# Two layers of a hybrid attention block: later turns of the attention outputs, the last two of them inside the first out-projection unit, and sums over the output weights taken three units ahead

## The chip, the cores and the metric

The kernel runs on one core of a Trainium2 chip. The metric is the device time of one execution in microseconds (us), the median of three runs. The profile below is of one further execution.

## What is computed

The reference is a backbone block of a latent generator, two layers deep, on 512 latent tokens and 256 context tokens of width 1024. Cut to what matters here:

```python
def trunk_layer(x, xt, ...):
    h  = modulate(rms_norm(x,  g_attn), sh_a,  sc_a)
    ht = modulate(rms_norm(xt, g_attn), tsh_a, tsc_a)
    q_w,k_w,v_w, q_n,k_n,v_n, q_g,k_g,v_g = split_mixer_inputs(h @ w_in, qk_g)     # groups A, B, C
    ...                                                  # the same for the context, rotary on A and C
    o = concatenate([window_attention(A), neighbourhood_attention(B), global_block_attention(C)])
    x = x + ga_a * (o @ w_out)                           # the output projection
    x = x + ga_f * swiglu(modulate(rms_norm(x, g_ffn), sh_f, sc_f), w_gate, w_up, w_down)
    if update_ctx:                                       # first layer only
        ot = concatenate([context_attention(A), context_attention(B), context_attention(C)])
        xt = xt + tga_a * (ot @ w_out)
        xt = xt + tga_f * swiglu(...)
    return x, xt
```

There are 16 heads of 64: A has 6 (windowed, with a sink logit), B has 4 (neighbourhood, with a bias), C has 6 (global). Layer 0 works on latent and context tokens (768), layer 1 on the latent ones alone (512).

## The kernel before, in words

The program is one instruction stream for each engine, written out by hand, with semaphores between the streams. Each layer goes through norm, input projection, attention, output projection and FFN. The change touches the attention and the output projection; the FFN behind them begins when the residual of the output projection is complete and normed.

**Attention** is a sequence of steps, each one query block of one head: 96 in layer 0 (0 to 23 group A on latent tokens, 24 to 35 A on the context, 36 to 59 C latent, 60 to 79 C and B on the context, 80 to 95 B latent) and 64 in layer 1 (0 to 23 A, 24 to 47 C, 48 to 63 B). For step g, PE computes scores (`score`, L1158 and L1159), DVE takes their top (`top_of`, L1940 for the bias of B, L1943), DVE in layer 0 (L1950) and POOL in layer 1 (L768) turn it into an offset, ACT takes the exponential (`softmax`, L1506), PE transposes the probabilities two steps later (`turn`, L1175), ACT and DVE split them into a high and a low half (`turned_high` L1528, `turned_low` L1957) and PE weighs the values four steps later (`weigh`, L1190 and L1192). After every fourth step DVE sums the group (`sum_outputs`, L1965 and L1969) and POOL writes its high and low half (L799, L804, L809) and so releases `o_ready`.

**Turns.** The output projection needs the attention outputs with channels on partitions, in eight tiles m of 128 channels. `turn_output` (L1207) transposes tile m on PE: 8 transposes for the latent part (part 0), 4 for the context part (part 1, layer 0 only), into one of three PSUM banks that the steps' own transposes use too. ACT copies them out in `take_turned` (L1564; for tiles 3 and 4, part 0, two copies that also permute, L1560) and releases `ot_taken`. The table `OUT_TURNS` gives each turn the step at which PE and ACT issue it, behind that step's own work. Tiles 0, 1, 2 hold group A, 3 and 4 group B, 5 to 7 group C.

**The output projection** has eight units j (an output tile of 128 columns), each of eight contraction tiles in the order `OUT_ORDER` (0, 1, 2, 5, 6, 7, 3, 4), six matmuls each in layer 0 and three in layer 1 (L1262). Its weights come as float32 and are split in two f16 halves with a scale of their own for each unit: ACT squares and sums unit j's weights (`square_out`, L1541), PE adds the sums over the partitions (`sum_out`, L1243; for the first `N_OUT_EARLY` units in one go, L1229), DVE makes the scale (`scale_out`, L1976 to L1982), ACT rounds the high half (`round_out`, L1548), POOL scales and subtracts for the low half (`split_out`, L716 and L719). Before the change the first three units are squared and rounded within the steps, and unit 0 is split by POOL among its last output writes; the rest follows during the units, `sum_out(j + 2)` behind the first tile of unit j. The raw weights of units 3 to 7 are loaded to where attention buffers were, once the last `o_ready` is out.

After unit 0 PE bounds the activations (L1267), and after units 2 and 3 it adds the weight sums of the first two FFN weight pairs (`sum_weights`, L1014), for which ACT squares in `first_pairs` (L1597), DVE scales in `scale_weights` (L2036 to L2043) and ACT rounds (L1608). DVE adds the residual (L1790) and the squares for the next norm (`add_square`, L1719), ACT squares the residual (L1386). The last unit's norm sums are on PE at L954 and L960. Before the first unit's own squares ACT switches its table and warms the root (L1589).

## Time and profile before

| | before |
|---|---|
| median of 3 runs | 1812.2 us (1811.83 to 1812.23) |
| profiled execution | 1816.11 us |
| its span in the trace | 1814.3 us |
| mean granted TensorE clock | 0.972 |
| PE busy | 1683.0 us (93%) |
| DVE, ACT, POOL busy | 964.3, 714.1, 835.0 us |
| attention, layer 0 (first exponential to last value matmul) | 226.9 to 431.2 us |
| output projection, layer 0 | 434.98 to about 501 us |
| attention, layer 1 | 1230.7 to 1379.6 us |
| output projection, layer 1 | 1383.38 to about 1436.6 us |

Busy time is not time at full speed: a matmul that is issued while the clock is at half its speed is busy twice as long. A table by stage therefore has the granted clock beside the busy times. "Idle before, released by" says how long an engine stood before a group and which semaphore let it go.

### The profile page before, as it was taken

The numbers are of one execution on the slowest core, as the hardware profiler recorded it, in microseconds if no ns is written. First come the engines' busy times: TensorE is split into PE (matmuls) and PEld (weight loads), VectorE is DVE, ScalarE is ACT, GpSimd is POOL, SyncE is SP. The second block draws the span as 40 slices with busy tenths as digits, with TensorE's granted clock in tenths as the row PEclk, the third lists the DMA queues.
The fourth block names the chain that finished last, engine by engine and source line by source line (L and its number), as shares of the span: only waits on it lengthen the run. The fifth ranks groups of instructions, "written<-read, shape, count | busy, mean of one in ns | idle before, by whom it ended". The sixth has DMA issues, their size and how long they took to land. (4 is left out here: it accounts for less than half of the span.)

```text
span 1814.3 us, 28248 instructions
## 1 busy us (share of the span) xinstructions
PE 1683.0 (93%) x11087; PEld 1201.4 (66%) x11087; DVE 964.3 (53%) x1760; ACT 714.1 (39%) x1276; POOL 835.0 (46%) x656
## 2 busy tenths in 40 slices
PE   7999988977989999999899989997976899999998
PEld 3688877865656678667766778786764345645646
DVE  4544498884468841787238743457883522122112
ACT  3222278877443310332013112226886464053130
POOL 2244347784514452436314234532444557458463
PEclk9999989998989999999999989999998899999999
DMA  9344352322134423363315423533003224334332
GB/s 312 49 113 113 96 137 78 89 64 76 37 95 137 129 67 85 100 178 101 110 48 180 128 64 73 120 88 91 11 13 94 58 70 116 93 89 109 82 81 82
DMA packets 314353, 175.01 MB, mean 96 GB/s; under 512 B 87518, under 2 KB 309614, under 8 KB 314222
## 3 DMA queue, kind: packets, MB, share of 16 engines
q1 hardware_dynamic: 284686, 143.70, 30.5%
q10 hardware_dynamic: 29536, 29.51, 5.1%
q8 instruction: 89, 1.46, 0.3%
q14 instruction: 42, 0.34, 0.1%
HBM read 159.04 MB, written 2.83 MB: 89 GB/s over the span
## 5 line engine op out<-in xcount | busy, mean ns | idle before, releaser
L981 PE MATMUL acc<-act,pair_w 128*128 128x512 f16 x3168 | 582.2, 345 | 6.2 <-ACT act L1403 4.2
L981 PEld LDWEIGHTS acc<-act,pair_w 128*128 128x128 f16 x3168 | 307.8, 98 | 270.6 <-DVE act L1765 10.0
L981 PE MATMUL acc<-hidden,split_w 128*128 128x512 f32 (+1 forms) x1584 | 311.8, 358 | 10.7 <-issue 6.4
L981 PEld LDWEIGHTS acc<-hidden,split_w 128*128 128x128 f32 x1584 | 261.9, 189 | 58.0 <-issue 7.1
L706 POOL TENSOR_SCALAR split_w<-raw_w 128x1024 fp32r<-128x1024 f32 (+1 forms) x104 | 109.2, 1050 | 354.9 <-PE acc L981 274.4
L843 POOL TENSOR_SCALAR pair_raw<-pair_raw,weight_scale 128x1024 f32<-128x1024 f32 x88 | 106.6, 1212 | 357.2 <-ACT pair_w L1608 357.2
L981 PE MATMUL acc<-act,split_w 128*128 128x512 f32 x1344 | 261.4, 353 | 4.1 <-ACT act L1403 2.5
L709 POOL TENSOR_TENSOR split_w<-raw_w,split_w 128x1024 fp32r<-128x1024 f32 (+1 forms) x104 | 241.9, 2326 | 8.7
L981 PEld LDWEIGHTS acc<-act,split_w 128*128 128x128 f32 x1344 | 214.1, 190 | 39.6 <-issue 3.6
L2109 DVE SCALAR_TENSOR_TENSOR mod_acc<-mod_chunk,silu_c,mod_acc 128x256 f32<-128x256 f32 x280 | 230.3, 865 | 4.0
L846 POOL TENSOR_TENSOR pair_w<-pair_raw,pair_w 128x1024 f16<-128x1024 f32 x88 | 189.0, 2148 | 7.3
L2072 DVE SCALAR_TENSOR_TENSOR prod<-acc,weight_scale,silu_g 128x768 f32<-128x768 f32 (+1 forms) x44 | 38.9, 884 | 256.4 <-PE acc L981 251.2
L1597 ACT ACTIVATE squares_out<-pair_raw 128x1024 bf16<-128x1024 f32 x88 | 92.6, 1052 | 170.4 <-DMA pair_raw<-in_w_up 166.1
L1790 DVE SCALAR_TENSOR_TENSOR x_t<-acc,mod,x_t 128x512 f32<-128x512 f32 x72 | 45.2, 659 | 207.5 <-PE acc L981 206.9
L1506 ACT ACTIVATE prob<-acc,stat,score_scale 128x768 f32<-128x768 f32 (+5 forms) x160 | 131.2, 820 | 54.2 <-DVE stat L1950 26.5
L1653 ACT ACTIVATE hidden<-prod 128x768 fp32r<-128x768 f32 (+1 forms) x44 | 32.4, 737 | 242.2 <-DVE prod L2072 242.2
L1943 DVE TENSOR_REDUCE stat<-acc 128x1 f32<-128x768 f32 (+5 forms) x160 | 117.3, 733 | 15.4 <-PE acc L1159 10.3
L1190 PE MATMUL small<-v,prob_t 128*128 128x128 f16 x696 | 83.4, 224 | 32.6 <-DVE o_sum L1969 31.5
L1262 PE MATMUL acc<-out,out_w 128*128 128x512 f16 x576 | 111.8, 355 | 1.0 <-POOL out_w L719 1.0
L1158 PE MATMUL acc<-ks,qs 128*128 128x256 f16 (+1 forms) x384 | 92.5, 272 | 20.0 <-ACT prob L1506 19.1
L1608 ACT ACTIVATE pair_w<-pair_raw,weight_scale 128x1024 f16<-128x1024 f32 x88 | 95.9, 1136 | 7.6 <-DVE weight_scale L2043 7.6
L1957 DVE TENSOR_TENSOR prob_t<-side,prob_t 128x512 f16<-128x512 f32 (+2 forms) x157 | 86.6, 567 | 21.4 <-ACT prob_t L1528 19.9
(216 smaller groups left out, 2141.9 us busy)
## 6 DMA issues: line engine op xcount, KB each, us to landing
mod_chunk<-in_w_mod ACTq DMA_DIRECT2D x28, 1024.0 KB, 5.2
pair_raw<-in_w_gate SPq DMA_DIRECT2D x44, 512.0 KB, 4.0
pair_raw<-in_w_up SPq DMA_DIRECT2D x44, 512.0 KB, 5.4
raw_w<-in_w_in SPq DMA_DIRECT2D x64, 256.0 KB, 3.7
raw_w<-in_w_down SPq DMA_DIRECT2D x32, 512.0 KB, 4.2
raw_w<-in_w_mod SPq DMA_DIRECT2D x24, 512.0 KB, 3.9
mod_start<-in_w_mod SPq DMA_DIRECT2D x8, 1024.0 KB, 11.4
ks<-q_split SPq DMA_DIRECT2D x64, 96.0 KB, 2.2
```

Of the source, the lines that this page charges most:

```text
L706: pool.tensor_scalar(split_w[slot][:, 0, 0:n, :], raw_w[slot][:, 0:n, :], 1.0, 0.0, ALU.mult, ALU.add).then_inc(hi_w, 1)
L709: pool.tensor_tensor(split_w[slot][:, 1, 0:n, :], raw_w[slot][:, 0:n, :], split_w[slot][:, 0, 0:n, :].bitcast(F32), ALU.subtract).then_inc ...
L843: pool.tensor_scalar(raw, raw, weight_scale[:, 1, 2 * f + s:2 * f + s + 1], 0.0, ALU.mult, ALU.add).then_inc(weight_mul, 1)
L846: pool.tensor_tensor(w[:, s, 1, :, :], raw, w[:, s, 0, :, :], ALU.subtract).then_inc(pair_ready, 1)
L981: mm = pe.matmul(acc[slot][:, a:b], weights[:, part == 2, k, :], moving[:, part == 1, k, a:b], start=(k == 0 and part == 0), stop=(k == n ...
L1158: pe.matmul(out_, q, ks[:, s["k"], 0, k0:k0 + size], start=True, stop=False)
L1262: mm = pe.matmul(acc[u % 2][:, a:b], out_w[j % 4][:, part == 2, k, :], out16[k][:, part == 1, a:b], start=(i == 0 and part == 0), stop=(i ...
L1506: sc.activation(prob[g % 3][:, 1 - s["sink"]:1 + n], src, ACT.Exp, bias=stat[:, 1, i:i + 1], scale=score_scale[:, 0, gi:gi + 1], accum_out ...
L1597: sc.activation(squares_out[:, :], pair_raw[home(f)][:, s, :, :].rearrange("p k n -> p (k n)"), ACT.Square, accum_out=weight_sum[:, 2 * f ...
L1608: sc.activation(pair_w[home(f)][:, s, 0, :, :], pair_raw[home(f)][:, s, :, :], ACT.Copy, scale=weight_scale[:, 1, 2 * f + s:2 * f + s + 1] ...
L1943: ve.reduce_max(stat[:, 0, i:i + 1], src, AX_X).then_inc(top, 1)
L2109: s = ve.scalar_tensor_tensor(**kw, in1=kw["out"], op0=ALU.mult, op1=ALU.add)
```

## The change: what it does, and the diff

It moves the turns of group A (tiles 0 to 2) from the C latent steps to the context steps in layer 0 and from the A and C steps to the first B steps in layer 1, and spreads the later ones anew. The turn of tile 3, part 0, now stands at the head of unit 0 and that of tile 4 in front of unit 0's seventh tile. Only two units' weights are summed together; in layer 1 their squares, scale, rounding and POOL's split now stand in the A steps, with a scratch tile of their own (`out_squares1`). The other sums stand one unit earlier: that of unit 2 behind unit 0's first tile, that of unit 3 in front of unit 0's seventh tile, that of unit j + 3 within unit j. The FFN's first two weight sums stand one unit later. The kernel's arithmetic is the same.

```diff
 OUT_TURNS = [
-    [(38, 0, 0), (40, 1, 0), (42, 2, 0), (47, 0, 1), (49, 1, 1), (51, 2, 1), (74, 5, 0), (75, 6, 0), (76, 7, 0),
-     (79, 5, 1), (83, 6, 1), (86, 7, 1), (90, 3, 1), (94, 4, 1), (99, 3, 0), (100, 4, 0)],
-    [(26, 0, 0), (29, 1, 0), (37, 2, 0), (50, 5, 0), (53, 6, 0), (60, 7, 0), (66, 3, 0), (68, 4, 0)],
+    [(60, 0, 0), (62, 1, 0), (64, 2, 0), (66, 0, 1), (68, 1, 1), (70, 2, 1), (74, 5, 0), (77, 6, 0), (80, 7, 0),
+     (82, 5, 1), (84, 6, 1), (87, 7, 1), (90, 3, 1), (95, 4, 1), (100, 3, 0), (100, 4, 0)],
+    [(48, 0, 0), (50, 1, 0), (52, 2, 0), (54, 5, 0), (57, 6, 0), (61, 7, 0), (68, 3, 0), (68, 4, 0)],
 ]
...
-OUT_SUM_STEP = [92, 56]
-OUT_SQUARE_STEP = [(88, 89, 90), (51, 52, 53)]
-OUT_ROUND_STEP = [(94, 95, 96), (58, 59, 61)]
-N_OUT_EARLY = 3
+OUT_SUM_STEP = [92, 6]
+OUT_SQUARE_STEP = [(88, 90), (2, 4)]
+OUT_ROUND_STEP = [(94, 97), (8, 10)]
+N_OUT_EARLY = 2
+N_OUT_SUMS = KT - N_OUT_EARLY + 1
...
+        out_squares1 = place("out_squares1", [P, 8 * P], BF16, split_at_ + 12288)
...
-            def split_out(l, j):
-
-                u = u_out(l) + j
+            def scale_raw(l, j):
+
                 pool.wait_ge(out_hi, KT * l + j + 1)
                 pool.tensor_scalar(out_raw[j][:, :, :], out_raw[j][:, :, :], out_scale[:, 1, j:j + 1], 0.0, ALU.mult, ALU.add
                                    ).then_inc(hi_w, 1)
+
+            def split_out(l, j):
+
+                u = u_out(l) + j
                 pool.wait_ge(hi_w, ring_of[u] + 1)
...
-                    if i == 4 * N_GROUPS[l]:
+                    if i == 14:
+                        scale_raw(l, 0)
+                    if i == 18:
                         split_out(l, 0)
...
-                for n, m, part in turns_at(l, g1 + 4 - g0):
-                    turn_output(n, m, part)
+                last_two = turns_at(l, g1 + 4 - g0)
 
                 def sum_out(j):
 
+                    if j == 2:
+                        pe.wait_ge(o_summed, sum(N_GROUPS[:l + 1]))
                     pe.wait_ge(out_sq, KT * l + j + 1)
...
                     for i, k in enumerate(OUT_ORDER):
+                        if j == 0 and i in (0, KT - 2):
+                            turn_output(*last_two[i // 6])
                         if j == 0:
                             pe.wait_ge(ot_taken, last_turn[k])
-                        if 1 <= j < KT - 2 and i == 1:
-                            sum_out(j + 2)
+                        if j == 0 and i in (1, KT - 2):
+                            sum_out(2 + i // 6)
+                        if 1 <= j < KT - 3 and i == 1:
+                            sum_out(j + 3)
...
-                    if j in (2, 3):
-                        sum_weights(l, j - 2)
+                    if j in (3, 4):
+                        sum_weights(l, j - 3)
...
-                    if j == 0:
+                    if l == 0 and j == 0 or l and j == 2:
                         sc.wait_ge(scores, LAYER_STEPS[l][-16] + 1)
+                    elif l and j == 0:
+                        sc.wait_ge(unit_done, u_in(l) + 16)
...
                     for n, m, part in turns_at(l, g - g0):
                         take_turned(n, m, part)
+                    if g == g1 + 1:
+                        square_out(2)
...
                 def first_pairs(k):
                     if k == 0:
+                        round_out(2)
                         square_out(3)
-                    elif k + 2 < KT:
-                        round_out(k + 2)
                     if k + 4 < KT:
                         square_out(k + 4)
-                    if k in (1, 2):
-                        square_pair(k - 1)
-                    if k in (4, 5):
-                        round_pair(k - 4)
+                    if k + 3 < KT:
+                        round_out(k + 3)
+                    if k in (2, 3):
+                        square_pair(k - 2)
+                    if k in (5, 6):
+                        round_pair(k - 5)
...
-                    if 1 <= j < KT - 2:
-                        scale_out(j + 2, j + 3, small[:, j + 2:j + 3])
+                    for i in ((2, 3) if j == 0 else (j + 3,) if j < KT - 3 else ()):
+                        scale_out(i, i + 1, small[:, i:i + 1])
...
-                    if j in (2, 3):
-                        scale_weights(j - 2)
+                    if j in (3, 4):
+                        scale_weights(j - 3)
```

**PE, end of the attention and unit 0 in layer 0, before.** The names are `out_0` to `out_7` for the eight turned tiles, `o` for the attention outputs, `out_w` for the split weights; "..." stands for the same six matmuls on the tiles between.

```order
L1207 MATMUL side<-ident_h,o_132 128x128 [waits o_ready,prob_lo]
L1207 MATMUL side<-ident_h,o_132 128x128 x7
L1207 MATMUL mod_ps<-ident_h,o_132 128x128 [waits o_ready,prob_lo]
L1207 MATMUL mod_ps<-ident_h,o_132 128x128 x7
L1262 MATMUL acc<-out_0_133,out_w_54 128x512 [waits ot_taken,split_ready,exps]
...
L1262 MATMUL acc<-out_1_134,out_w_54 128x512 [waits ot_taken]
...
L1262 MATMUL acc<-out_4_137,out_w_54 128x256
L1267 MATMUL mod_ps<-act_scale,ones 128x1 [waits bound_step]
L1262 MATMUL acc<-out_0_133,out_w_55 128x512 [waits split_ready]
...
L1243 MATMUL small<-out_sum,ones_69 128x1 [waits out_read,out_sq]
```

The same place after the change:

```order
L1216 MATMUL side<-ident_h,o_132 128x128 [waits ot_taken,o_ready,split_ready,exps]
L1216 MATMUL side<-ident_h,o_132 128x128 x7
L1276 MATMUL acc<-out_0_133,out_w_54 128x512 [waits ot_taken]
...
L1253 MATMUL small<-out_sum,ones_69 128x1 [waits out_sq,out_read,o_summed,ot_taken]
L1276 MATMUL acc<-out_1_134,out_w_54 128x512
...
L1276 MATMUL acc<-out_7_140,out_w_54 128x512 [waits ot_taken]
...
L1216 MATMUL mod_ps<-ident_h,o_132 128x128 [waits o_ready,prob_lo]
L1216 MATMUL mod_ps<-ident_h,o_132 128x128 x7
L1253 MATMUL small<-out_sum,ones_69 128x1 [waits out_read,out_sq,ot_taken]
L1276 MATMUL acc<-out_3_136,out_w_54 128x512
```

Tile 4's turn has moved behind the matmuls of six tiles, and directly behind it, ahead of tile 3's matmuls, PE now executes the sum for unit 3, which waits for ACT's squares (`out_sq`).

**ACT, from the last softmax steps of layer 0 to the first units, before:**

```order
L1564 ACTIVATE out_4_137<-side,o_scale 128x2x256 [waits ot_ps]
L1548 ACTIVATE out_w_54<-raw_w_50,out_scale 128x1024 [waits unit_done,out_scaled]
...
L1548 ACTIVATE out_w_55<-raw_w_51,out_scale 128x1024 [waits unit_done,out_scaled]
L1528 ACTIVATE prob_t_110<-mod_ps 128x512 [waits prob_ps,o_ps]
L1548 ACTIVATE out_w_56<-out_raw_141,out_scale 128x1024 [waits unit_done,out_scaled]
L1528 ACTIVATE prob_t_111<-side 128x512 [waits prob_ps,o_ps]
L1560 ACTIVATE out_3_136<-side,o_scale 128x64x8 [waits ot_ps]
...
L1560 ACTIVATE out_4_137<-mod_ps,o_scale 128x64x8 [waits ot_ps]
...
L1589 ACT_TABLE_LOAD
...
L1541 ACTIVATE out_squares,out_sum<-out_raw_142 128x1024 [waits out_sq,out_raw_in3]
```

and after the change:

```order
L1581 ACTIVATE out_4_137<-side,o_scale 128x2x256 [waits ot_ps]
L1542 ACTIVATE prob_t_110<-mod_ps 128x512 [waits prob_ps,o_ps]
L1542 ACTIVATE prob_t_111<-side 128x512 [waits prob_ps,o_ps]
L1558 ACTIVATE out_squares,out_sum<-out_raw_141 128x1024 [waits out_sq,out_raw_in2]
L1565 ACTIVATE out_w_55<-raw_w_51,out_scale 128x1024 [waits unit_done,out_scaled]
L1577 ACTIVATE out_3_136<-side,o_scale 128x64x8 [waits ot_ps]
...
L1577 ACTIVATE out_4_137<-mod_ps,o_scale 128x64x8 [waits ot_ps]
...
L1608 ACT_TABLE_LOAD
...
L1565 ACTIVATE out_w_56<-out_raw_141,out_scale 128x1024 [waits unit_done,out_scaled]
L1558 ACTIVATE out_squares,out_sum<-out_raw_142 128x1024 [waits out_sq,out_raw_in3]
```

The roundings of units 1 and 2 no longer stand between the last two `turned_high`; the squares of unit 3 (`out_raw_142`) come behind the copy of tile 4, the table load and now also the rounding of unit 2.

**POOL, the last steps of layer 1, before:**

```order
L799 TENSOR_TENSOR o_132<-o_sum_119,stat 128x4x64 [waits r_denom,o_summed]
L716 TENSOR_SCALAR raw_w_50<-raw_w_50,out_scale 128x1024 [waits out_hi]
L719 TENSOR_TENSOR out_w_54<-raw_w_50,out_w_54 128x1024 [waits hi_w]
L804 TENSOR_TENSOR o_sum_119<-o_sum_119,stat 128x256 [waits o_hi]
L809 TENSOR_TENSOR o_132<-o_sum_119,o_132 128x4x64 [waits o_mul]
L799 TENSOR_TENSOR o_132<-o_sum_118,stat 128x4x64 [waits r_denom,o_summed]
```

After the change these two stand among the offsets of the A steps (L773 is the old L768):

```order
L773 TENSOR_SCALAR stat<-stat,score_scale 128x1 [waits top]
L717 TENSOR_SCALAR raw_w_50<-raw_w_50,out_scale 128x1024 [waits out_hi]
L773 TENSOR_SCALAR stat<-stat,score_scale 128x1 [waits top]
...
L814 TENSOR_TENSOR o_132<-o_sum_119,o_132 128x4x64 [waits o_mul]
L773 TENSOR_SCALAR stat<-stat,score_scale 128x1 [waits top]
L724 TENSOR_TENSOR out_w_54<-raw_w_50,out_w_54 128x1024 [waits hi_w]
L773 TENSOR_SCALAR stat<-stat,score_scale 128x1 [waits top]
```

The end of layer 1's attention has lost them; SP's order of loads is the same in both kernels.

## Rows read from the trace of the kernel before

**Rows 1.** Stages of layer 0's attention: busy us (count), clock, DMA share, GB/s.

```profile
core 0: us, PE busy (x) PEld busy (x) DVE busy (x) ACT busy (x) POOL busy (x), PEclk, DMA share, GB/s
309.40:342.50 33.10, 31.31 (x405) 28.45 (x403) 27.12 (x55) 27.50 (x64) 22.74 (x20) 1.00 0.32 89
342.50:362.60 20.10, 18.72 (x243) 17.12 (x241) 17.14 (x37) 16.13 (x39) 16.04 (x15) 1.00 0.30 85
369.20:373.86 4.66, 3.10 (x36) 2.38 (x34) 4.35 (x16) 3.67 (x13) 3.29 (x6) 1.00 0.42 118
379.30:384.97 5.67, 3.85 (x54) 3.19 (x53) 4.19 (x15) 5.51 (x15) 5.43 (x9) 1.00 0.34 95
```

**Rows 2.** Timeline of PE, last turns and unit 0 of layer 0; start us, us.

```profile
430.98 1.04 PE L1207 MATMUL side<-ident_h,o 128*128 128x128 f16 x8
434.18 1.01 PE L1207 MATMUL mod_ps<-ident_h,o 128*128 128x128 f16 x8 [2.16 <-POOL o L809]
434.98 9.85 PE L1262 MATMUL acc<-out,out_w 128*128 128x512 f16 x48
```

**Rows 3.** Timeline of ACT, the same stretch.

```profile
427.92 1.16 ACT L1548 ACTIVATE out_w<-out_raw,out_scale 128x1024 f16<-128x1024 f32 x1
...
432.06 4.85 ACT L1560 ACTIVATE out<-side,o_scale 128x512 f16<-128x512 f16 x2 [2.50 <-PE side L1207]
436.40 5.12 ACT L1560 ACTIVATE out<-mod_ps,o_scale 128x512 f16<-128x512 f16 x2
441.53 1.28 ACT L1589 ACT_TABLE_LOAD   x1
...
442.94 1.04 ACT L1541 ACTIVATE out_squares<-out_raw 128x1024 bf16<-128x1024 f32 x1
```

**Rows 4.** Windows of layer 0's output projection, columns as in rows 1.

```profile
434.90:436.00 1.10, 1.10 (x6) 0.53 (x5) 0.00 (x0) 1.10 (x1) 1.02 (x2) 0.50 0.23 60
438.00:440.00 2.00, 2.00 (x11) 1.10 (x10) 0.00 (x0) 2.00 (x2) 1.92 (x2) 0.80 0.46 134
444.70:501.00 56.30, 56.30 (x359) 34.31 (x357) 23.79 (x55) 24.12 (x32) 30.59 (x18) 1.00 0.25 60
```

**Rows 5.** Windows of layer 1: attention stages, output projection; columns as in rows 1.

```profile
1230.00:1262.00 32.00, 21.72 (x225) 18.31 (x226) 25.55 (x47) 20.10 (x47) 7.28 (x14) 0.89 0.40 98
1284.30:1302.60 18.30, 16.05 (x200) 13.99 (x198) 15.71 (x28) 16.27 (x34) 7.28 (x17) 1.00 0.01 2
1302.60:1311.00 8.40, 7.75 (x98) 6.93 (x97) 7.99 (x15) 7.24 (x17) 5.61 (x12) 1.00 0.01 2
1337.00:1372.50 35.50, 22.62 (x277) 19.37 (x275) 28.36 (x57) 29.23 (x59) 10.98 (x26) 1.00 0.04 11
1391.50:1436.60 45.10, 39.66 (x181) 17.07 (x179) 18.32 (x48) 22.29 (x32) 22.35 (x14) 0.96 0.36 85
```

**Rows 6.** Line L1564, take of a turn on ACT: min/median/max ns.

```profile
L1564 ACT ACTIVATE out<-mod_ps,o_scale x11: 662/1106/1129, 304.6 to 1366.4; 128x1024 f16<-128x1024 f16 x8, 128x512 f16<-128x512 f16 x3
```

**Rows 7.** Timeline of POOL, last groups of layer 1.

```profile
1373.12 1.13 POOL L716 TENSOR_SCALAR raw_w<-raw_w,out_scale 128x1024 f32<-128x1024 f32 x1
1374.33 2.12 POOL L719 TENSOR_TENSOR out_w<-raw_w,out_w 128x1024 f16<-128x1024 f32 x1
1376.41 0.62 POOL L804 TENSOR_TENSOR o_sum<-o_sum,stat 128x256 f32<-128x256 f32 x1
```

**Rows 8.** Timeline of PE, unit 0 of layer 1 and the first FFN sum.

```profile
1382.58 1.01 PE L1207 MATMUL side<-ident_h,o 128*128 128x128 f16 x8 [3.01 <-POOL o L809]
1383.38 7.49 PE L1262 MATMUL acc<-out,out_w 128*128 128x512 f16 x24
...
1404.80 0.16 PE L1014 MATMUL mod_ps<-weight_sum,ones 128*128 128x2 bf16 x1 [3.38 <-DVE act_bound L2022]
```

**Rows 9.** Timeline of DVE in layer 1, two operations beside POOL's L719, one without.

```profile
1375.44 0.69 DVE L1957 TENSOR_TENSOR prob_t<-side,prob_t 128x512 f16<-128x512 f32 x1 [0.89 <-ACT prob_t L1528]
...
1403.89 0.69 DVE L1719 TENSOR_TENSOR inv<-inv,sq 128x512 f32<-128x512 f32 x1 [6.89 <-ACT sq L1386]
...
1416.07 2.38 DVE L1719 TENSOR_TENSOR inv<-inv,sq 128x512 f32<-128x512 f32 x1 [2.13 <-ACT sq L1386]
```

More of the change, by code:

```diff
@@ L412, in trunk @@
         o_hi, o_mul = sem("o_hi"), sem("o_mul")
-        out_raw_in = [sem(f"out_raw_in{j}") for j in range(N_OUT_EARLY - 1, KT)]
+        out_raw_in = [sem(f"out_raw_in{j}") for j in range(2, KT)]
         out_sq, out_ps, out_read, out_back, out_scaled = (
@@ L461, in out_call @@
         def out_call(l, j):
-            return 6 * l + max(0, j - N_OUT_EARLY + 1) + 1
+            return N_OUT_SUMS * l + max(0, j - N_OUT_EARLY + 1) + 1
         def width(l):
@@ L848, in _ @@
                 for j in range(1, KT):
+                    scale_raw(l, j)
                     split_out(l, j)
@@ L899, in free_bank @@
                 elif kind == "w":
-                    pe.wait_ge(out_read, 6 * c + 1)
+                    pe.wait_ge(out_read, N_OUT_SUMS * c + 1)
                 elif c < len(ATTN_MOD):
@@ L1536, in square_out @@
                         sc.wait_ge(out_raw_in[j - 2], 96 * (l + 1))
-                    if j == 0:
+                    if l == 0 and j == 0 or l and j == 2:
                         sc.wait_ge(scores, LAYER_STEPS[l][-16] + 1)
+                    elif l and j == 0:
+                        sc.wait_ge(unit_done, u_in(l) + 16)
                     if l or j:
                         sc.wait_ge(out_sq, KT * l + j)
-                    sc.activation(out_squares[:, :], out_raw[j][:, :, :].rearrange("p k n -> p (k n)"), ACT.Square,
+                    scratch = out_squares1 if l and j < 2 else out_squares
+                    sc.activation(scratch[:, :], out_raw[j][:, :, :].rearrange("p k n -> p (k n)"), ACT.Square,
                                   accum_out=out_sum[:, j:j + 1]).then_inc(out_sq, 1)
```

3 lines of the change are left out of this document (2 added, 1 removed).

## The prediction

> **What bounds the kernel now.** I read the shares of the engines first: PE is busy for 93% of the span. So time is lost or won where PE waits or runs at half clock, and in the attention, where PE, DVE and ACT take turns at being the bound. Next I read the windows by stage. In the C latent steps of layer 0 PE is full (31.31 of 33.10 us); on the context DVE is nearly so (4.35 of 4.66) and with turns ACT (5.51 of 5.67) [rows 1]. In layer 1 the A stage leaves every engine some room, the B stage has ACT and DVE side by side at 29.23 and 28.36 of 35.50 us [rows 5]. Then the timelines at the seam between attention and output projection [rows 2, 3, 7, 8]: there PE waits for the last outputs (2.16 and 3.01 us) and runs unit 0 at half clock: the window from 434.90 is granted 0.50, that from 438 0.80, and everything from 444.70 on 1.00 [rows 4]. 0.50 is the lower level, 1.2 GHz, which PE had after the sparse last steps. From 444.70 PE is busy for 56.30 of 56.30 us: in layer 0 nothing in the projection can be gained by earlier weights, while any delay ahead of it goes through whole. In layer 1 PE is busy for 39.66 of 45.10, and one wait of 3.38 us stands at the first FFN sum [rows 5, 8].
>
> **The change part by part**, against the profiled execution; the median of the runs lies 3.9 us below it, so the sum is added to 1812.2.
>
> *Layer 0, C latent steps lose six turns.* Twelve steps with five of the turns took 33.10 us, eight without 20.10, or 2.51 a step [rows 1]: the five cost 33.10 - 30.15 = 2.95, part of it being modulation work that the first window has slightly more of. I take **-2.6** for all six; bounds -1.5 (modulation is half of it) and -3.5 (2.95 x 6/5).
>
> *The context steps get them.* Four steps without a turn took 4.66 us, four with two full turns 5.67 [rows 1], so 0.5 for a full turn and about 0.27 for a half: 3 x 0.5 + 3 x 0.27 = 2.3, less 0.5 for tile 7, which leaves for the B steps: **+1.8** (0.5 if the takes fit in ACT's gaps, 3.6 if each costs ACT's 1.1 us [rows 6]).
>
> *Layer 0, B steps.* One square (1.04, and some 0.1 to read its sum [rows 3]) goes, one full turn comes at 0.5: **-0.6** (-1.5 to +0.3).
>
> *Layer 0, unit 0: the large term.* Roundings of 1.16 us [rows 3] no longer stand between the last `turned_high`, which I count as 0.9 earlier for the whole tail: tile 3's turn at 430.1, unit 0 at 430.9 instead of 434.98 [rows 2]. A tile takes 0.98 at full clock (56.30 us for 56 tiles and the norm sums) and 1.95 at half. Before, the clock rose about 4.7 us after PE took up work at 434.18 [rows 2, 4]; I let it rise at 435.6. Then 2.4 tiles at half and 3.6 at full clock end at 439.1, and tile 4's turn at 439.6. Now the new wait: behind that turn PE meets `sum_out(3)`, which needs ACT's squares of unit 3, and queued in front of these on ACT are tile 4's copy, the table, a rounding. By rows 3: copy 4.85 with its reaction, to 444.6; table and root 1.4 (441.53 to 442.94), to 446.0; rounding 1.05, to 447.1; square 1.13, to 448.3. PE stands idle for 8.7 us, as do tile 3 and all units queued behind it. Two tiles are left, 1.96, and half clock behind so long a pause, which I price as before at half of 4.4 us, 2.2: unit 0 ends at 452.5, where it ended at 434.98 + 9.85 = 444.83 [rows 2]. **+7.7**, passed on whole, since PE has no slack behind it [rows 4]. Bounds: +5.5 (no half clock behind the pause) and +10 (twice as long).
>
> *Layer 1, A steps.* They get squares, a scale on DVE, roundings and POOL's pair. DVE (25.55 of 32.00) is nearest to full [rows 5] and I count its scale at face, 0.7 (three small dependent operations, nearest: the 0.69 of rows 9); ACT has 12 us free for 4 x 1.1, of which 0.9 shows; POOL's 2.12 behind an offset delays the next offset once, 0.6. **+2.2** (0.7 to 4.5: only DVE's part, or ACT's four whole). POOL's subtraction also lies beside DVE work. Beside L719 `prob_t`, which reads PSUM, took 0.69, its usual time; but `add_square` took 0.69 without and 2.38 with it [rows 9], 1.7 more. From step 14 on DVE runs only reductions and `prob_t`, so I add nothing; were one operation hit, the term would be 1.7 more. The Trainium skill's page "SBUF — State Buffer", section "Who interferes with whom", says that a DVE instruction with two SBUF inputs contends with a GpSimd instruction that reads SBUF and one with at most one does not; rows 9 agree, and by the page too only an operation of the first kind would pay here.
>
> *Layer 1, C steps lose three turns.* Eight steps with two took 18.30, four without 8.40 [rows 5]: 0.75 each, **-2.2** (-1.2 to -3.3, PE's part alone to ACT's 1.1 each).
>
> *Layer 1, B steps.* Out: three squares and three roundings, 6 x 1.1 = 6.6, and DVE's scale 0.7; in: three turns, 3.3 [rows 3, 6]. Net 4.0 on engines that are busy for 80% of the stage, **-3.5** (-1.5 if ACT's 6 us of idle time held part of it, -5.0 if DVE's share also tells).
>
> *Layer 1, seam and projection.* POOL's pair, 1373.12 to 1376.41, goes from ahead of the last outputs [rows 7]. Tile 3's turn had to follow its group's last POOL steps, which ran from 1376.41; without the pair I put it at 1376.8, and unit 0 begins right behind it, at 1377.6, no longer behind tile 4's turn at 1382.58 [rows 8]. A tile is two thirds of layer 0's: 0.65, at half clock 1.3. 2.7 tiles to 1381.1, 3.3 more to 1383.3, turn 1383.8, copy 1388.7, table, rounding and square as above to 1392.3: the same pause, 8.5 us. Two tiles 1.3 and 2.2 for the clock: 1395.8 for the end of unit 0, before 1390.87. The rest, 7 x 5.2 and 1.2 for the norm sums, ends at 1433.4 against 1436.6, since sums a unit earlier and FFN sums a unit later leave no reason for the 5.4 us that PE did not work there, the 3.38 at L1014 among them [rows 5, 8]. **-3.2** (-5.2 without loss of clock, -0.5 if half of these waits come back, for instance at POOL's splits).
>
> *No cost of its own:* the scratch tile, and the loads, whose order on SP is the same; the loads of units 3 to 7 start with the last `o_ready`, a little earlier, beside unit 0. If they came late, unit 3 would wait, not unit 0.
>
> Sum: layer 0 -2.6 + 1.8 - 0.6 + 7.7 = +6.3; layer 1 +2.2 - 2.2 - 3.5 - 3.2 = -6.7; together -0.4, **1811.8 us**: gain and loss cancel. The profiled execution would be 1815.7. About 0.2%, 3.6 us, is what a measurement of this kernel can tell from no change.
>
> **Rivals.**
>
> *Slower: the pauses cost the clock more than I count.* Place: the pause in front of unit 0's seventh tile in both layers. PE is idle for 8.7 us behind a first stretch that itself began at half clock. For it: after the last B steps, in which PE was busy in scraps, 0.50 still held at 434.90 [rows 4]; unit 0 now starts four to six us sooner and so may only have its rise at the old instants. Against: once PE worked without pause it had the full clock in under 5 us. Price: first stretch at half clock to 439, +1.7, and in layer 1 all six tiles, +2.1; behind the pause 10 us at half instead of 4.4, +2.8, and +1.0 in layer 1, whose units have slack. Together +7.6, **1819.4 us**. It decides the sign once the extra comes to 4.0 us.
>
> *Faster: layer 1's attention gives more.* With the weight work out, the B stage falls to DVE's own load: 28.36 busy less 0.7 and little idle, 29.5 instead of 35.5, -6 in place of -3.5; and the additions in the A stage vanish in room that is there (ACT 20.10 of 32.00), 0 in place of +2.2 [rows 5]. Together -4.7, **1807.1 us**. Against: the stages hand work round in steps, and no stage here runs as short as its busiest engine.
>
> *A DVE operation with two SBUF inputs is caught beside POOL's moved pair:* +1.7 once, 1813.5, still no change that can be told. The page named above states the rule; the order of the changed DVE stream speaks against it.
>
> *The change does not do what it says.* The order rows shown above leave no doubt on the place of the new wait: the sum for unit 3 stands directly behind tile 4's turn. If ACT's squares were there by then, the pauses would be 3 to 5 us shorter in each layer, around 1804.
>
> **How the numbers follow.** Forecast 0.38, caught operation 0.05, slower rival 0.27, faster rival 0.27, no pause 0.03. The first two are "same", 0.43; with the extras on either side: faster 0.30, same 0.43, slower 0.27. The range goes from 1806 to 1819: it takes in the faster rival and nearly all of the slower one, and leaves some 0.07 out below and 0.12 above. The bounds added up would give -11 to +14, but they would have to err together.
>
> **What would show it.** In PE's timeline of either layer a pause of 8 to 9 us before unit 0's seventh tile, released by ACT's square (L1558), and the granted clock behind it; the end of unit 0 near 452 less what the attention gained; no wait of 3 us at the first FFN sum of layer 1; the stages of rows 1 and 5 shorter and longer as priced. A pause under 5 us, PE released by something else, or a B stage of layer 1 that keeps its 35 us would make the prediction wrong.

## The result: slower by about a quarter of a per cent, and where the profile after has it

| | before | changed |
|---|---|---|
| median of 9 runs | 1812.23 us (1811.22 to 1815.58) | 1816.97 us (1814.51 to 1822.6) |
| ratio, 95% interval | | 1.0026 (1.0014 to 1.0037) |
| later series | 1813.69 us (35 runs) | 1816.88 us (12 runs), ratio 1.0020 (1.0005 to 1.0034) |
| profiled execution, its span | 1816.11 us, 1814.3 | 1814.51 us, 1812.1 |
| granted clock, mean | 0.972 | 0.975 |

The forecast was 1811.8 us and no change that can be told; measured was 4.7 us more than before. The two traces alone would have said the opposite of the medians: that of before belongs to an execution 3.9 us above its median, that of the changed kernel to the fastest of nine. In what follows "before" is short for the kernel before the change. So both kernels were traced once more (the first two experiments), and what follows compares stages, each with two traces on either side.

The page of the changed kernel has the same shares as before:

```profile
PE 1677.8 (93%) x11089; PEld 1199.3 (66%) x11089; DVE 956.5 (53%) x1766; ACT 714.5 (39%) x1276; POOL 834.7 (46%) x656
```

Windows of the changed kernel, cut some 0.5 us behind the starts of the exponentials (L1520) of layer 0's steps 36, 60, 72, 80, 95 and layer 1's 0, 24, 48, 63, the last one ending early in the FFN; columns as in [rows 1]:

```profile
299.40:358.70 59.30, 56.21 (x718) 51.72 (x716) 51.65 (x107) 47.98 (x117) 44.93 (x38) 1.00 0.32 88
358.70:379.90 21.20, 15.61 (x199) 12.88 (x195) 14.71 (x46) 16.60 (x49) 11.36 (x12) 1.00 0.18 52
379.90:392.90 13.00, 9.04 (x110) 7.59 (x110) 9.46 (x30) 9.53 (x29) 12.44 (x17) 1.00 0.15 42
392.90:427.10 34.20, 25.89 (x297) 22.62 (x297) 29.91 (x69) 27.24 (x63) 17.15 (x24) 0.95 0.17 48
1237.60:1293.10 55.50, 41.81 (x480) 35.78 (x481) 45.29 (x90) 41.14 (x94) 19.10 (x37) 0.94 0.31 70
1293.10:1343.60 50.50, 46.20 (x567) 40.75 (x565) 47.87 (x85) 43.41 (x96) 28.40 (x59) 1.00 0.03 7
1343.60:1378.20 34.60, 25.00 (x294) 21.80 (x293) 27.79 (x55) 26.24 (x53) 10.93 (x27) 0.95 0.03 9
1378.20:1455.40 77.20, 62.69 (x318) 29.38 (x319) 36.62 (x78) 46.73 (x61) 42.02 (x31) 0.89 0.37 89
```

The same stages in the second trace of the kernel before, cut some 0.4 us behind the starts:

```profile
299.00:362.00 63.00, 58.85 (x750) 53.49 (x748) 52.12 (x106) 51.81 (x122) 44.95 (x39) 1.00 0.31 84
362.00:378.80 16.80, 13.07 (x167) 11.25 (x165) 14.50 (x46) 12.78 (x42) 11.09 (x12) 1.00 0.22 64
378.80:391.10 12.30, 9.14 (x116) 7.79 (x114) 9.73 (x30) 10.99 (x31) 11.74 (x17) 1.00 0.16 45
391.10:425.30 34.20, 25.48 (x293) 22.69 (x293) 29.81 (x69) 27.21 (x64) 18.14 (x24) 0.95 0.17 47
1230.40:1282.80 52.40, 41.61 (x477) 35.70 (x478) 44.96 (x87) 37.32 (x88) 16.25 (x35) 0.94 0.33 74
1282.80:1335.60 52.80, 47.62 (x588) 41.92 (x587) 47.84 (x84) 46.14 (x99) 28.35 (x59) 1.00 0.02 7
1335.60:1371.20 35.60, 26.15 (x275) 23.05 (x275) 28.66 (x58) 29.35 (x59) 11.00 (x27) 0.86 0.03 9
1371.20:1453.90 82.70, 65.50 (x316) 29.71 (x317) 36.08 (x75) 44.79 (x59) 44.86 (x33) 0.86 0.34 83
```

The reader is to see in the ACT column of the second window that it grew by 3.8 us (12.78 to 16.60), and the window by 4.4: what the moved turns add to ACT comes out at full price. Worked out in the same way from all traces. The "seam" is the end of the attention behind its last exponential; layer 0's seam and projection are taken up to the residual of the last unit (L1810, before L1790), layer 1's up to a matmul early in the FFN:

| stage, us | before, two traces | changed, two traces | difference | forecast |
|---|---|---|---|---|
| L0 C latent, steps 36 to 59 | 63.1, 63.1 | 59.3, 59.3 | -3.8 | -2.6 |
| L0 context, steps 60 to 79 | 29.1, 29.1 | 34.2, 35.7 | +5.1, +6.6 | +1.8 |
| L0 B, steps 80 to 95 | 34.2, 34.2 | 34.2, 34.2 | 0 | -0.6 |
| L0 seam and projection | 76.2, 76.4 | 82.3, 82.4 | +6.1 | +7.7 |
| L0 FFN to L1's first step | 728.6, 728.7 | 728.2, 730.2 | +0.6 | 0 |
| L1 A, steps 0 to 23 | 53.6, 52.4 | 55.5, 54.8 | +2.2 | +2.2 |
| L1 C, steps 24 to 47 | 52.9, 52.9 | 50.5, 50.5 | -2.4 | -2.2 |
| L1 B, steps 48 to 63 | 35.5, 35.5 | 34.6, 34.8 | -0.8 | -3.5 |
| L1 seam and projection | 83.0, 82.7 | 77.2, 77.8 | -5.4 | -3.2 |

With the rest (-0.7 ahead of step 36, some +0.4 behind the last window) the means of the two pairs differ by about +2, and the four profiled times give (1814.51 + 1818.70 - 1816.11 - 1813.21) / 2 = +1.9. The medians differ by 4.7 and, in the later series, by 3.2. Each profiled execution of before is slower than the median of its own runs (1812.23 and 1811.28), so some 1 to 3 us of the result lie in what a usual execution of before saves against these two, and that isn't seen.

**Unit 0 of layer 0.** PE's timeline of the changed kernel:

```profile
431.83 0.62 PE L1216 MATMUL side<-ident_h,o 128*128 128x128 f16 x8
432.30 1.14 PE L1276 MATMUL acc<-out,out_w 128*128 128x512 f16 x6
433.27 0.17 PE L1253 MATMUL small<-out_sum,ones 128*128 128x1 bf16 x1
433.30 5.04 PE L1276 MATMUL acc<-out,out_w 128*128 128x512 f16 x30
438.17 0.61 PE L1216 MATMUL mod_ps<-ident_h,o 128*128 128x128 f16 x8
447.32 0.16 PE L1253 MATMUL small<-out_sum,ones 128*128 128x1 bf16 x1 [8.54 <-issue]
447.34 4.00 PE L1276 MATMUL acc<-out,out_w 128*128 128x512 f16 x12
```

and ACT's beside it:

```profile
438.82 4.81 ACT L1577 ACTIVATE out<-mod_ps,o_scale 128x512 f16<-128x512 f16 x2 [1.43 <-PE mod_ps L1216]
443.64 1.28 ACT L1608 ACT_TABLE_LOAD   x1
...
445.05 1.13 ACT L1565 ACTIVATE out_w<-out_raw,out_scale 128x1024 f16<-128x1024 f32 x1
446.09 1.04 ACT L1558 ACTIVATE out_squares<-out_raw 128x1024 bf16<-128x1024 f32 x1
447.03 0.18 ACT L1558 ACTIVATION_READ_ACCUMULATOR out_squares<-out_raw 128x1 f32 x1
```

The pause is there, 8.54 us long. The trace puts it down to "issue", not to ACT; but ACT has read out the sum of its square at 447.21, 0.11 us before PE goes on at 447.32, and the queue in front of it is copy, table, rounding, square. The second trace has the same pause, 8.54 us. Windows of the same trace show the clock: before the pause 1.00, late in it and behind it 0.50.

```profile
434.00:438.00 4.00, 4.00 (x26) 2.38 (x25) 0.62 (x4) 3.39 (x2) 3.84 (x4) 1.00 0.20 57
442.60:447.30 4.70, 0.00 (x0) 0.01 (x1) 0.00 (x0) 4.59 (x6) 1.02 (x1) 0.50 0.86 234
447.30:451.20 3.90, 3.88 (x14) 1.90 (x15) 0.48 (x3) 2.19 (x3) 3.73 (x4) 0.50 1.16 216
452.80:456.20 3.40, 3.40 (x24) 2.09 (x23) 0.62 (x4) 2.68 (x4) 0.75 (x2) 1.00 0.56 157
```

Layer 1 has the same pause, 8.80 us, in front of the sum at 1395.46; the wait of [rows 8] at the first FFN sum has gone from 3.38 to 0.34 us:

```profile
1386.04 0.61 PE L1216 MATMUL side<-ident_h,o 128*128 128x128 f16 x8
1395.46 0.16 PE L1253 MATMUL small<-out_sum,ones 128*128 128x1 bf16 x1 [8.80 <-issue]
```

### The profile page after: what moved, and what is told of

Same layout as the page of the kernel before. It is cut to its first block and busy times, and to the rows that moved or that the text cites. A ratio compares the mean times of both kernels' runs of the same rounds, so it can differ in the third digit from the quotient of the medians.

```text
span 1812.1 us, 28262 instructions
## 1 busy us (share of the span) xinstructions
PE 1677.8 (93%) x11089; PEld 1199.3 (66%) x11089; DVE 956.5 (53%) x1766; ACT 714.5 (39%) x1276; POOL 834.7 (46%) x656
## 5 line engine op out<-in xcount | busy, mean ns | idle before, releaser
L2129 DVE SCALAR_TENSOR_TENSOR mod_acc<-mod_chunk,silu_c,mod_acc 128x256 f32<-128x256 f32 x280 | 224.0, 842 | 4.0
L1810 DVE SCALAR_TENSOR_TENSOR x_t<-acc,mod,x_t 128x512 f32<-128x512 f32 x72 | 45.2, 658 | 211.9 <-PE acc L990 211.4
L1520 ACT ACTIVATE prob<-acc,stat,score_scale 128x768 f32<-128x768 f32 (+5 forms) x160 | 130.9, 818 | 60.5 <-DVE stat L1970 31.0
L1668 ACT ACTIVATE silu_g<-acc,weight_scale 128x768 f32<-128x768 f32 (+1 forms) x44 | 34.6, 787 | 148.8 <-PE acc L990 113.5
```

The costliest lines, as they stand in the source:

```text
L1520: sc.activation(prob[g % 3][:, 1 - s["sink"]:1 + n], src, ACT.Exp, bias=stat[:, 1, i:i + 1], scale=score_scale[:, 0, gi:gi + 1], accum_out ...
L2129: s = ve.scalar_tensor_tensor(**kw, in1=kw["out"], op0=ALU.mult, op1=ALU.add)
```

## The experiments

**Second traces of both kernels.** No edit.

> The kernel before, unchanged, for a second trace and for the spread of its runs. The medians say the change costs 4.7 us, the two traces say -0.4 at the last residual, and the trace of before belongs to an execution 3.9 us above its median. Theory 1 (the two profiled executions were untypical in places the change does not touch): time 1811 to 1816 us, and in a trace near 1812 the 4 us are missing in one place outside attention end and out-projection. Theory 2 (they lie in the granted clock at the seams): the stretches at half clock around unit 0 of one of the layers come out shorter by some 4 us in it.

> The changed kernel, unchanged, for a second trace. Its profiled execution was the fastest of nine, 1814.5 against a median of 1817.0. Theory 1: 1814 to 1819 us, with the 2 to 4 us above the first trace outside the changed places. Theory 2 (the pause in unit 0 costs the clock a varying amount): PE runs at half clock for longer behind the pause of 8.5 us in one of the layers, and unit 0 or 1 ends 2 to 4 us later than in the first trace.

Measured: 1811.28 us (12 runs) and 1816.88 us (12 runs). The profiled executions took 1813.21 and 1818.70. The first figure is also a measure of the noise: the same kernel's 35 other runs of that series have 1813.69, so two medians of one kernel lie 2.4 us apart (ratio 0.9990, interval 0.9978 to 1.0001). Neither theory had it right alone. Of the 2.3 us between the last residuals of the two traces of before, 1.2 are in layer 1's A steps and 0.7 ahead of layer 0's step 36. Between the two of the changed kernel, 2.6 us at the last residual, the second is longer by 2.0 in the FFN and the next input projection of layer 0, by 1.5 in steps 72 to 79 and by 0.6 in layer 1's seam, and shorter by 1.2 ahead of step 36 and by 0.7 in layer 1's A steps. In steps 72 to 80 the reason shows: the window from 378.70 of the second trace is granted 0.88, while its counterpart above was granted 1.00.

```profile
378.70:393.20 14.50, 10.50 (x110) 8.85 (x110) 9.60 (x30) 9.59 (x29) 13.78 (x20) 0.88 0.13 38
```

Layer 0's C latent steps and steps 60 to 71 and layer 1's C steps, in which the clock stays at 1.00 in all four traces, repeat to 0.1 us from trace to trace of a kernel. That is what makes the stage table usable where the medians, with a spread of 10 us, are not.

**The sum moved back to unit 1, then tile 4's turn earlier as well.** DVE's scale for unit 3 moves with the sum, and the sum for unit 4 stands three tiles later in unit 1.

```diff
-                        if j == 0 and i in (1, KT - 2):
-                            sum_out(2 + i // 6)
-                        if 1 <= j < KT - 3 and i == 1:
+                        if j == 0 and i == 1:
+                            sum_out(2)
+                        if j == 1 and i == 1:
+                            sum_out(3)
+                        if 1 <= j < KT - 3 and i == (4 if j == 1 else 1):
                             sum_out(j + 3)
...
-                    for i in ((2, 3) if j == 0 else (j + 3,) if j < KT - 3 else ()):
+                    for i in ((2,), (3, 4), (5,), (6,), (7,), (), (), ())[j]:
```

> The sum for unit 3's weights stands in unit 1 again, the rest of the change stays. The pause in front of tile 3 goes; PE then runs tile 3 (1 us) and waits for ACT's copy of tile 4, 4.85 us from its turn, so some 4 us of pause are left in each layer, and about 1.5 at the sum in unit 1. If the pause is what the change loses: 3 to 5 us less than the changed kernel in each layer, in all 1809 +-2 against 1817. If the loss lay in the attention or elsewhere (theory 1): less than 2 us gained.

The second kernel adds this:

```diff
-                        if j == 0 and i in (0, KT - 2):
-                            turn_output(*last_two[i // 6])
+                        if j == 0 and i in (0, 2):
+                            turn_output(*last_two[i // 2])
```

> As the last, and tile 4's turn in front of unit 0's third tile instead of its seventh: ACT's copy is then covered by four tiles of matmuls, and only a wait of 2 to 3 us at unit 1's sum for unit 3 is left. Pause theory: 7 to 9 us less than the changed kernel in layer 0 and 4 to 8 in layer 1, 1802 to 1806 us. Rival (the later weights then bound the units, since loads and POOL's splits keep their times): no more than 2 us below the kernel with the sum alone moved.

Measured: 1811.62 us (ratio to before 0.9988, interval 0.9976 to 1.0000) and 1811.55 us (0.9989, 0.9977 to 1.0002). So the place of one sum takes back 5 us of the changed kernel's time. Neither kernel can be told from before, whose own 12 runs had 0.9990. By stages: layer 0's seam and projection go from 82.4 to 77.7 and 74.4, against 76.3 before the change. (The trace with 74.4 has the clock at 1.00 all the way from 425 to 500 us; the kernel of 1806.35 us below has the same code there, two stretches of 3.4 us at half clock, and 75.5.) Layer 1's go from 77.5 (mean) to 76.4 and 77.2 only: there the pause costs about 1 us, or 2 if the stage is ended with the projection's last matmul (60.3 and 58.3 us). So the first expectation came out in layer 0 (4.7 less, 3 to 5 expected) and not in layer 1, and its median lies 0.6 us above its range. In PE's timeline of the first kernel the pause in layer 1 is split in two, and the first is the expected one, for ACT's copy of tile 4:

```profile
1391.84 1.46 PE L1278 MATMUL acc<-out,out_w 128*128 128x512 f16 x3 [3.74 <-ACT out L1579]
1395.43 0.19 PE L1253 MATMUL small<-out_sum,ones 128*128 128x1 bf16 x1 [0.61 <-ACT out_squares L1560]
1402.54 0.18 PE L1253 MATMUL small<-out_sum,ones 128*128 128x1 bf16 x1 [0.59 <-ACT out_squares L1560]
```

The second expectation came out in layer 0 (8.0 less, 7 to 9 expected) and failed in layer 1 (0.3 less, 4 to 8 expected), and its median did not fall below the first kernel's; its trace has layer 0's seam shorter by 3.3 us, layer 1's A stage longer by 1.0 and its seam by 0.8. PE's timeline of layer 1 shows why:

```profile
1385.28 1.46 PE L1278 MATMUL acc<-out,out_w 128*128 128x512 f16 x3 [3.10 <-ACT out L1579]
...
1396.87 0.18 PE L1253 MATMUL small<-out_sum,ones 128*128 128x1 bf16 x1 [2.59 <-ACT out_squares L1560]
```

The wait for the copy shrinks only from 3.74 to 3.10 us, and that of the sum in unit 2 grows from 0.59 to 2.59: ACT's square there had itself waited 4.05 us for the load of its weights. So the rival, that later weights hold the units, holds for layer 1.

**One part of the change undone at a time**, the rest as changed. Group A's turns of layer 0 back (`OUT_TURNS[0]` begins `(38, 0, 0), (40, 1, 0), (42, 2, 0), (47, 0, 1), (49, 1, 1), (51, 2, 1)` again), group A's turns of layer 1 back (`(26, 0, 0), (29, 1, 0), (37, 2, 0)`), and the early weights of layer 1 back:

```diff
-OUT_SUM_STEP = [92, 6]
-OUT_SQUARE_STEP = [(88, 90), (2, 4)]
-OUT_ROUND_STEP = [(94, 97), (8, 10)]
+OUT_SUM_STEP = [92, 56]
+OUT_SQUARE_STEP = [(88, 90), (51, 52)]
+OUT_ROUND_STEP = [(94, 97), (58, 59)]
...
-                    if i == 14:
-                        scale_raw(l, 0)
-                    if i == 18:
+                    if i == 4 * N_GROUPS[l]:
+                        scale_raw(l, 0)
                         split_out(l, 0)
```

> The changed kernel with group A's six turns of layer 0 back in the C latent steps (38 to 51), nothing else undone. Theory 1 (a take is 1.1 us, or 0.7 for a half, on ACT between two links of a short context step's chain, and shows at face there, while a C step hides a third of it): C latent steps 3.8 us longer again, context steps 5 to 6 us shorter, net 1 to 3 us faster than the changed kernel. Rival (the context stage grew by something else, the clock or the later steps 77 to 82): the context steps keep more than 3 us of their growth, and the kernel is slower than the changed one.

> The changed kernel with group A's three turns of layer 1 back at steps 26, 29, 37. Theory 1 (a take costs about the same wherever it stands): C steps 2.4 us longer, B steps 2.5 to 3 shorter, net within 0.6 us. Rival (the B steps are short because the weight work is gone, and turns cost nothing there): B steps within 0.5 us of the changed kernel, net 2 us slower.

> The changed kernel with the sums, roundings and POOL's split of layer 1's first units back in the B steps. By my forecast A steps would be 2.2 us shorter, B steps 3.5 + 3 longer and the seam 3.3 longer. By the trace, where the B stage won only 0.8 us with three turns in it: A steps 2 to 3 shorter, B steps 3 to 4 longer, seam 3 longer; net 3 to 5 us slower than the changed kernel. Rival (early weights are a wash): within 1 us.

Measured, stages of the profiled executions in us. "L1 seam" is layer 1's seam and projection. The first two rows have both traces of each kernel, and medians of the first series, for before those of its 12 and of its 35 other runs; the series of the last three rows gave before 1813.7 as well.

| kernel | median | L0 C | L0 60-71 | L0 72-79 | L1 A | L1 C | L1 B | L1 seam |
|---|---|---|---|---|---|---|---|---|
| before | 1811.3, 1813.7 | 63.1 | 16.7 | 12.4 | 53.6, 52.4 | 52.9 | 35.5 | 83.0, 82.7 |
| changed | 1816.9 | 59.3 | 21.2 | 13.0, 14.5 | 55.5, 54.8 | 50.5 | 34.6, 34.8 | 77.2, 77.8 |
| turns0_old | 1815.0 | 63.1 | 16.7 | 14.5 | 55.8 | 50.6 | 34.8 | 77.1 |
| turns1_old | 1817.1 | 59.3 | 21.2 | 13.0 | 53.5 | 52.9 | 32.0 | 76.5 |
| weights1_late | 1819.9 | 59.3 | 21.2 | 15.1 | 52.3 | 50.5 | 36.9 | 78.8 |

The six turns of layer 0 cost 3.8 in the C latent steps and 4.5 in the context steps; moving them loses 0.7, and theory 1 stands for these twelve steps, though not for the 5 to 6 it gave. The median, 1.9 us below the changed kernel's, is no evidence: the intervals overlap (0.9993 to 1.0032 against 1.0005 to 1.0034). Steps 26, 29 and 37 are C steps; the change took no turn out of layer 1's A steps. The three turns cost 2.4 in the C steps and 2.7 in the B steps: a wash, as theory 1 said. The early weights save 2.2 in the B steps and 1.3 at the seam and cost some 2.9 in the A steps: a wash too, the rival's case. (The A steps are the least certain of these: over all fourteen traces they take 53.2 to 56.3 us with the early weights and 51.7 to 53.6 without, at granted clocks from 0.86 to 0.97.) The median of weights1_late (6 runs, 3 us above the changed kernel) isn't borne out by these stages; its profiled execution was 1.6 and 2.8 us later than the changed kernel's two already before step 36, and the last experiment repeats the question on a better base.

**One part of the change alone:** the kernel before with group A's turns of layer 0 at steps 60 to 70.

> The kernel before with one part of the change alone: group A's six turns of layer 0 at steps 60 to 70. Theory (the take stands at face in the chain of the short steps): steps 36 to 60 shorter by 3.7 us, steps 60 to 72 longer by 4.5, everything else as before but for the clock: 0 to +2 us against the kernel before. Rival (the gain in the C steps outweighs it): 1 us or more faster. Beside it: whether the half clock at the end of the context steps, seen in five of eight traces with the moved turns of tiles 6 and 7 and in neither trace of before, comes with these six turns.

Measured: 1816.52 us, ratio 1.0014 (1.0001 to 1.0027). Its windows, C latent, steps 60 to 71, steps 72 to 79:

```profile
300.10:359.40 59.30, 56.20 (x718) 51.66 (x715) 51.62 (x107) 47.92 (x117) 44.95 (x39) 1.00 0.32 89
359.40:381.60 22.20, 17.00 (x199) 14.20 (x196) 14.79 (x46) 16.56 (x48) 11.32 (x12) 0.92 0.17 49
381.60:394.00 12.40, 9.11 (x115) 7.78 (x114) 9.84 (x30) 11.12 (x31) 11.84 (x17) 1.00 0.15 44
```

-3.8 and +4.5, and one more us in a window that was granted 0.92, 5.5 in all, where before had 1.00. The theory holds for the twelve steps and the median, 2.3 us above before in its series (1814.24), is just past its 0 to +2; the rival fell. Stretches at half clock come with moved turns: in steps 60 to 71 in this trace and in that of the first kernel above, and in steps 72 to 79 in five of the eight traces with tiles 6 and 7 turned at steps 77 and 80, one of which (turns0_old) has group A's turns at their old places. The five traces with all these turns as before have none. That the stretches follow from the turns is likely, not shown.

**Group A's turns as before in both layers, with sum and tile 4's turn as in the second kernel above;** then also the turns of tiles 5 to 7 of layer 0 as before (75, 76, 79, 83, 86), while those of layer 1 stay moved; then the sums for units 3 and 4 two and three tiles later in unit 1 (`i == 3` and `i == 7`).

> Sum for unit 3 in unit 1, tile 4's turn before unit 0's third tile, and the turns of group A in both layers where they were before. Adds the gain of turns0_old and turns1_old to that of the kernel with sum and turn moved, 1811.6: 1809 to 1811 us, 2 to 5 below the kernel before. Rival (what is left over is clock, given and taken at random): same as the kernel before within 1 us.

> early_turn_old_turns (1810.0 us) with the turns of tiles 5 to 7 of layer 0 also where they were before (75, 76, 79, 83, 86). Theory (every full take costs 1 us wherever it lies in a short step): steps 72 to 80 shorter by 0.7, steps 80 to 95 within 0.3, total 0 to 1 us faster. Rival (the new places draw a stretch at half clock at the end of the context steps): up to 2 us faster in the median.

> As early_turn_all_old_turns, with the sums for units 3 and 4 two or three tiles later in unit 1. Theory (PE meets the sum before ACT's squares are there and waits 1.5 to 3 us, in both layers): the wait at unit 1's sums goes, 1 to 2 us faster in layer 0, where PE has no other slack; in layer 1 nothing, since POOL's splits and DVE's scales then hold the units. Rival (the later scale delays rounding and split of unit 3): PE waits the same time at the head of unit 3.

Measured: 1810.04 us (ratio 0.9979, 0.9967 to 0.9992), **1806.35 us (0.9964, 0.9951 to 0.9977)** and 1806.84 us (0.9968, 0.9955 to 0.9981). The second beats both kernels of this study: its context steps have before's 16.7 and 12.4, its B stage of layer 1 31.7, its seam there 76.6, and layer 0's seam 75.5. The first came out as expected. Between the first and the second, steps 72 to 79 are shorter by 0.6 as expected and layer 0's B steps by 0.8, more than expected; that the median fell by 3.7 is more than the theory and the rival gave, and is not shown to be real, since the intervals overlap and the profiled executions took 1806.73 and 1807.39. PE timeline of the second, layer 0:

```profile
441.80 1.15 PE L1278 MATMUL acc<-out,out_w 128*128 128x512 f16 x6 [1.92 <-ACT out L1579]
...
445.39 0.19 PE L1253 MATMUL small<-out_sum,ones 128*128 128x1 bf16 x1 [0.43 <-ACT out_squares L1560]
```

In the third the sums of unit 1 wait no more in layer 0, and unit 2's waits instead, for squares whose load ACT itself had waited 4.41 us for. Its theory fell (layer 0's seam and projection 77.0, not shorter than 75.5), and so did its rival, which had named unit 3's head.

```profile
451.69 0.18 PE L1253 MATMUL small<-out_sum,ones 128*128 128x1 bf16 x1 [2.29 <-ACT out_squares L1560]
```

**The early weights once more,** late in the kernel of 1806.35 us (the diff of weights1_late).

> early_turn_all_old_turns (1806.4 us) with squares, sums, roundings and POOL's split of layer 1's first two units back in the B steps. By stages: A steps of layer 1 shorter by 2.5 (0.8 in steps 4 to 8, 1.7 in steps 8 to 12) and up to 1.3 more that goes with the clock; B steps longer by 2.0, the seam by 0.9 where POOL's split stands among the last outputs. Theory (the early weights are a wash): within 1 us of 1806.4. Rival 1 (they carried the gain in layer 1): 3 us slower, as the medians of weights1_late and the changed kernel stood. Rival 2 (they cost more in the A steps than they save): 1 us or more faster.

Measured: 1806.28 us, ratio 0.9968 (0.9956 to 0.9980), against 0.9964. A stage 51.7 for 56.0, B stage 34.6 for 31.7, seam 79.5 for 76.6, together 1.5 more. The theory holds: the early weights are a wash within what six runs of each can tell, some 2 us. That the 3 us of weights1_late were the spread of its few runs is then likely, not shown.

## Why the prediction was wrong

**The pause, right in place and size.** Forecast 8.7 and 8.5 us, measured 8.54 and 8.80, behind the queue of copy, table, rounding and square that the sum listed. Unit 0 of layer 0 cost +6.1 rather than +7.7, since the clock rose at 431.9 and 434.5 in the two traces, not at 435.6 (counted from tile 3's turn, as the 4.7 us of before were, the forecast's rise would be 434.8), so most of the six tiles ran at full speed; behind the pause PE ran at half clock until 452.4 and 451.5, for 5.1 and 2.7 us, so that 2.5 and 1.4 were lost where 2.2 was counted. The slower rival's mechanism, that unit 0 would run on at half clock to 439, did not happen, though its side of the result did.

**The step that failed: the price of a turn in the context steps, +1.8.** The sum took 0.5 us for a full turn from the four steps 72 to 75, with two turns, against the four steps 64 to 67, without [rows 1]. Measured were 4.5 us for three full and three half turns, which is what ACT's takes (its copies of a turned tile) add up to end to end, 3 x 1.0 + 3 x 0.57 = 4.7. Why the window misled can be seen in ACT's timeline of before, first steps 66 and 67 without a turn, then 74 and 75 with one each:

```profile
370.93 0.57 ACT L1506 ACTIVATE prob<-acc,stat,score_scale 128x256 f32<-128x256 f32 x1 [0.16 <-DVE stat L1950]
...
371.84 0.57 ACT L1506 ACTIVATE prob<-acc,stat,score_scale 128x256 f32<-128x256 f32 x1
...
373.59 0.57 ACT L1506 ACTIVATE prob<-acc,stat,score_scale 128x256 f32<-128x256 f32 x1 [0.82 <-DVE stat L1950]
...
381.11 0.57 ACT L1506 ACTIVATE prob<-acc,stat,score_scale 128x256 f32<-128x256 f32 x1 [0.16 <-DVE stat L1950]
...
381.67 1.10 ACT L1564 ACTIVATE out<-side,o_scale 128x1024 f16<-128x1024 f16 x1
...
382.93 0.57 ACT L1506 ACTIVATE prob<-acc,stat,score_scale 128x256 f32<-128x256 f32 x1
...
383.47 1.12 ACT L1564 ACTIVATE out<-mod_ps,o_scale 128x1024 f16<-128x1024 f16 x1
...
384.78 0.57 ACT L1506 ACTIVATE prob<-acc,stat,score_scale 128x256 f32<-128x256 f32 x1
```

Step 66 takes 0.91 us and step 74 takes 1.82: that turn costs 0.91. Step 67, the last of its group of four, takes 1.75 without a turn, because ACT waits 0.82 us for DVE, which sums the group's outputs (L1969, 0.66 us) ahead of the next step's offset; step 75, in the same place, takes 1.85: that turn costs 0.10, since its take fits into the wait. The 0.5 is the mean of the two. The changed kernel puts its six turns at steps 60, 62, 64, 66, 68 and 70, none of which is the last of a group of four, where that wait stands. Its twelve steps 60 to 71 are longer than before's by 0.73, 0, 1.06, 0.15, 0.91, 0.10, 0.48, 0.10, 0.48, 0.10, 0.23 and 0.14 us. In steps 64, 66 and 68 ACT's operations follow one another without a gap from one exponential to the next, so there the take itself is the delay; in the others PE's transposes may have a part, which no run separates. Turns at steps 63, 67 or 71 were not tried. The upper bound, 3.6, was too low as well: the sum's own prices, 1.1 and the 0.66 of [rows 6] for a half, less 1.1 for tile 7, give 4.2.

Steps 72 to 79 were forecast at -0.5, for tile 7's turn, and came out at +0.6, although tile 5's half turn leaves them too, which the sum overlooked: step 76 is shorter by 0.91 without its turn, step 77 longer by 1.55 with tile 6's. In the second trace 1.5 us more come with a stretch at half clock, for which the sum had no term. In place of +1.8: +5.1 and +6.6. Of the error of 4.1 in the mean, 2.2 are the price of group A's turns, 1.1 tiles 5 to 7, and the rest the clock.

**The second: layer 1's B steps, -3.5.** The additions were rightly priced (3.3 forecast, 2.7 measured by turns1_old), the removals not: squares, roundings and scale were taken at ACT's and DVE's busy time, 7.3, and gave 35.5 + 2.7 - 34.7 = 3.5; weights1_late agrees, with 2.2 for two of the three units. The likely reason, which no run tests by itself: a square has nobody waiting for it in the steps and fits in part into ACT's idle time of [rows 5], while a take stands between two links of the chain. The smallest gain that was allowed, -1.5, also missed -0.8. The faster rival rested on the same mistake.

**The others.** C latent -3.8 for -2.6, beyond its bound of -3.5: the same underpricing of a turn, here with the better sign. A steps +2.2 as forecast; no operation of DVE was caught: beside POOL's moved pair its `prob_t` took 0.69 us and its `top_of` 0.68, no more than elsewhere in the stage. C steps -2.4 for -2.2.

Layer 1's seam, -5.4 for -3.2, compares two different stretches. The forecast ended with the projection's last matmul; from step 63's exponential to there the traces have 64.1 and 63.4 us before, 60.0 and 60.6 after, so -3.5 for -3.2. The other 1.9 lie between there and the FFN, where both traces of before have the half clock for 10.2 us and both of the changed kernel for 6.8; the sum had no term for it. The hit of -3.5 is partly luck: unit 0 ended 2.8 and 2.3 us earlier than forecast against that exponential, since its first six tiles ran at full clock, and the units behind it took 39.5 us instead of 37.6. Taking the sum away from unit 0 gives back only 1 to 2 us in this layer, as sum3_unit1 shows, since the units behind used to wait anyway.

The errors: +4.1 in the context steps, +2.7 in layer 1's B steps, +0.6 each in layer 0's B steps and in the FFN, against -1.2, -1.6 and -2.2 in the C latent steps and the two seams and -0.6 in the rest. That is +2.4 on a forecast of -0.4, close to the +1.9 of the traces; the medians have 3 to 5. What in a usual execution of before is faster than in its two traces stays open. That the time measured, 1816.97 us, lies inside the stated 1806 to 1819 us is no merit of the sum: the gain and the loss that were to cancel did not. Its bounds added up give -11.8 to +13.7, not -11 to +14.

## What to carry to other kernels

Price a moved operation by where it stands in the chain, not by its engine's busy share: the same copy cost 0.91 us in a step whose engine had no gap and 0.10 in one whose engine waited anyway. So compare a step with its like in the pattern, not with a mean over neighbours, and ask whether the new place has the wait that hid the operation at the old one. End a measured stage where the forecast ended it. Where single runs spread by more than the effect, cut traces into stages: those with an undisturbed clock repeated to 0.1 us here and told parts of the change apart that the medians could not.
